# Hybrid diffusion step on one Trainium2 core: modulation row products moved behind whole weight pieces, the expert selection turned with its weights, overflow weights loaded from an earlier point

## The reference

```python
def adaln(cvec, w_mod, b_mod):
    m = jax.nn.silu(cvec) @ w_mod + b_mod
    return [t[:, None, :] for t in jnp.split(m, 6, axis=-1)]

hid = jax.nn.silu(jnp.einsum('nd,edf->nef', x, wg)) * jnp.einsum('nd,edf->nef', x, wu)
y = jnp.einsum('nef,efd->nd', hid * combine[..., None].astype(hid.dtype), wd)
```

## Time and profile before

| | us |
|---|---|
| median of three runs | 2106.62 (2103.02 to 2111.81) |
| the profiled execution, own time | 2109.68 |
| its span | 2107.9 |
| TensorE busy | 1938.4 (92%) |
| VectorE busy | 492.7 (23%) |
| ScalarE busy | 365.7 (17%) |
| mean granted TensorE clock | 0.956 of full |
| weight transfers | 593.40 MB, mean 282 GB/s |

### The profile page before, as it was taken

How to read it: one execution, slowest core, us unless ns; L and a number is a source line. 1 busy time by engine, 2 the same in 40 slices (tenths; PEclk the granted TensorE clock), 3 DMA queues, 4 the chain that set the end, 5 groups by cost and what they waited for, 6 DMA issues and landing times.

```text
span 2107.9 us, 23590 instructions
## 1 busy us (share of the span) xinstructions
PE 1938.4 (92%) x9696; PEld 1154.9 (55%) x9696; DVE 492.7 (23%) x1235; ACT 365.7 (17%) x735; POOL 15.0 (1%) x41
## 2 busy tenths in 40 slices
PE   5877999999999998999999997999999869999987
PEld 2445645545736766855554665744554547555543
DVE  1014411104300322231112334321112042311111
ACT  1013200003103321210002223300002042100002
POOL 1000000000000000000000000000000000000000
PEclk9988999999999978999999997999999988999988
DMA  9882389995997311549999672449999653499970
GB/s 328 311 314 106 153 365 427 428 421 215 351 353 272 120 40 58 201 175 427 428 427 397 235 271 80 180 200 424 429 428 361 228 216 128 163 425 428 428 302 21
DMA packets 126144, 593.40 MB, mean 282 GB/s; under 512 B 8008, under 2 KB 15312, under 8 KB 101088
## 3 DMA queue, kind: packets, MB, share of 16 engines
q1 hardware_dynamic: 115728, 585.12, 69.7%
q10 hardware_dynamic: 9840, 6.52, 1.1%
q0 software_dynamic: 480, 0.39, 0.1%
HBM read 587.29 MB, written 4.73 MB: 281 GB/s over the span
## 4 chain that ended last, share of the span: by engine, by line
PE 85%; DVE 5%; DMA 5%; ACT 4%; issue 2%; ACTq 0%; DVEq 0%; SPq 0%
PE PS L808 24%; PE PS L1249 21%; PE PS L1229 11%; PE PS L1260 10%; PE PS L837 4%; DMA ring<-in_moe_wu 2%; DMA ring<-in_w_mod 2%; PE PS L858 2%; PE PS L989 2%; PE PS L852 2%; ACT arena L591 1%; PE PS L1205 1%; PE PS L873 1%; DVE RS L1385 1%; PE PS L1144 1%
## 5 line engine op out<-in xcount | busy, mean ns | idle before, releaser
L1249 PE MATMUL PS<-ring,arena 128*64 128x512 f32 x1568 | 352.2, 594 | 6.7 <-ACT arena L741 4.3
L1229 PE MATMUL PS<-arena 128*128 128x128 f32 (+3 forms) x1584 | 252.1, 316 | 10.8 <-ACT arena L741 4.4
L1229 PEld LDWEIGHTS PS<-arena 128*128 128x128 f32 (+1 forms) x1584 | 221.3, 194 | 51.9 <-issue 25.0
L808 PE MATMUL PS<-H,ring 128*128 128x256 f32 (+1 forms) x1088 | 248.1, 383 | 1.6 <-DVE SQ L1454 1.6
L1249 PEld LDWEIGHTS PS<-ring,arena 128*64 128x64 f32 x1568 | 119.3, 137 | 231.4 <-issue 226.9
L1260 PE MATMUL PS<-ring,arena 128*64 128x512 f32 x1040 | 235.6, 597 | 4.0 <-DVE arena L1686 4.0
L808 PEld LDWEIGHTS PS<-H,ring 128*128 128x128 f32 x1088 | 203.5, 194 | 54.0 <-issue 28.4
L741 ACT ACTIVATE arena<-PS 128x512 f32<-128x512 f32 (+2 forms) x131 | 71.4, 545 | 899.4 <-PE PS L1260 362.0
L1706 DVE SCALAR_TENSOR_TENSOR arena<-arena,PS 128x512 f32<-128x512 f32 x32 | 35.3, 1104 | 533.4 <-PE PS L1249 533.4
L808 PE MATMUL PS<-arena,ring 128*128 128x256 f32 (+1 forms) x672 | 149.8, 385 | 5.4 <-DVE arena L1529 3.1
L1260 PEld LDWEIGHTS PS<-ring,arena 128*64 128x64 f32 x1040 | 73.0, 137 | 142.1 <-issue 133.5
(11 more groups left out here) (303 smaller groups left out, 1353.7 us busy)
## 6 DMA issues: line engine op xcount, KB each, us to landing
ring<-in_moe_wu SPq DMA_DIRECT2D x65, 2048.0 KB, 16.6
ring<-in_moe_wd SPq DMA_DIRECT2D x65, 2048.0 KB, 11.3
ring<-in_w_mod SPq DMA_DIRECT2D x48, 2048.0 KB, 17.9
ring<-in_moe_wg SPq DMA_DIRECT2D x33, 2048.0 KB, 18.7
arena<-in_moe_wg SPq DMA_DIRECT2D x32, 2048.0 KB, 19.2
ring<-in_mlstm_w_in SPq DMA_DIRECT2D x12, 2048.0 KB, 9.0
ring<-in_attn_w_qkv SPq DMA_DIRECT2D x6, 2048.0 KB, 20.4
ring<-in_gla_w_in SPq DMA_DIRECT2D x6, 2048.0 KB, 10.7
```

The costliest lines, as they stand in the source:

```text
L808: ins = mm(out, a, b, start=first and i == 0, stop=final and i == len(pairs) - 1)
L1229: return mm(out, rows, onehot, start=first, stop=final, skip_group_check=True)
L1249: ins = mm(PS[64 * e:64 * e + 64, b, :], XG[:, k, 64 * e:64 * e + 64], w[:, k], start=(k == 0), stop=(k == KD - 1))
```

## The change

- `MODS[3]` takes 12 pieces (before 8) and `MODS[4]` 4 (before 8): the GLA computes the first eight column blocks of layer 3's modulation, layer 3's attention only the last four.
- `fill` is gone. `mod_run(g, lo, hi)` issues row products after whole weight pieces: in layer 0's attention four after the key/value piece and four after the first query piece; in the mLSTM two after each of eight pieces; in the GLA two after each of six.
- In both attention layers the last four products stand between `scores(0)` and `scores(1)`; `mod_cols` stands after `scores(1)`, ScalarE's `mods` after `probs(0)`, VectorE's after the second maxima.
- In the GLA `mod_cols(3)` and `mods(3)` stand after the eight block products.
- The order of pieces follows: in layer 3 all three `qkv` pieces come before the four modulation pieces.
- `turn_w` transposes WB in place of PB; the two one-column matmuls go, `WTS` has no weight column, and `hid` is a plain product. `scatter` so applies the routing weight.
- The overflow's `wg` and `wu` go to the ring slots that pair 6's `wg` pieces leave, its `wd` to EXTRA's first place (`XWD`). SyncE waits for pair 6's and pair 7's first `up` and no longer for pair 7's second `up` and its `down`.

```diff
-MODS = [ORDER[a:b] for a, b in ((0, 4), (4, 16), (16, 32), (32, 40), (40, 48))]
+MODS = [ORDER[a:b] for a, b in ((0, 4), (4, 16), (16, 32), (32, 44), (44, 48))]
+GMODS = (0, 2, 4, 6, 8, 10, 12)
...
-                chunks += [("gin", 2, c)] + ([("mod", *u) for u in MODS[3][2 * c:2 * c + 2]] if c < 4 else [])
+                chunks += [("gin", 2, c)] + [("mod", *u) for u in MODS[3][GMODS[c]:GMODS[c + 1]]]
...
-            chunks += [("qkv", 3, 2)] + mod(3, 4, 8) + [("qkv", 3, 0)] + mod(3, 8, 12) + [("qkv", 3, 1)] + [("wo", 3, c) for c in range(2)]
+            chunks += [("qkv", 3, c) for c in (2, 0, 1)] + mod(3, 8, 12) + [("wo", 3, c) for c in range(2)]
...
+        XWD = ar(9608, 4, 1024)
...
-                    for j in range(3):
-                        wait(sp, *used(n - 6 + 2 * j))
+                    wait(sp, *used(n - 12))
+                    wait(sp, *used(n - 11))
+                    wait(sp, *used(n - 6))
...
-                            sp.dma_start(slot_view(w, (n - 6 + 2 * j) % RING), expert_weights(w, l, e)).then_inc(S(f"x_landed{j}"), 16)
+                            dst = XWD if w == "wd" else slot_view(w, (n - 6 + j) % RING)
+                            sp.dma_start(dst, expert_weights(w, l, e)).then_inc(S(f"x_landed{j}"), 16)
...
                 probs(0)
+                mods(l + 1)
...
+            def mod_run(g, lo, hi):
+
+                for i in range(lo, hi):
+                    mod_rows(g, i)
...
-                        if fill[m] and k == KD // 2:
-                            mod_rows(*fill[m])
...
+                if l == 0:
+                    mod_run(1, 0, 4)
...
+                    if l == 0 and m == 3:
+                        mod_run(1, 4, 8)
...
-                mod_cols(l + 1)
...
                 scores(0)
+                mod_run(l + 1, len(MODS[l + 1]) - 4, len(MODS[l + 1]))
                 for g in range(KV):
                     n = 4 * a + g
                     if g + 1 < KV:
                         scores(g + 1)
+                    if g == 0:
+                        mod_cols(l + 1)
...
+                    mod_run(2, 2 * c, 2 * c + 2)
...
+                    mod_run(2, 8 + 2 * c, 10 + 2 * c)
...
+                    mod_run(3, GMODS[c], GMODS[c + 1])
...
+                    if s:
+                        mod_run(3, GMODS[2 + i // 2], GMODS[3 + i // 2])
-                mod_cols(3)
...
+                    if i % 4 == 3:
+                        mod_run(3, GMODS[4 + i // 4], GMODS[5 + i // 4])
...
+                mod_cols(3)
                 pe.wait_ge(S("g_r_sb"), 8)
-                pe.wait_ge(S("mod"), mod_done(3))
...
                 def turn_w(b, sem, rows=P):
                     for s in range(2):
-                        tp(PS[0:rows, b, T * s:T * s + T], PB[:, s].rearrange("p e t -> p (e t)")[:, 0:rows], ident)
-                    for s in range(2):
-                        ins = mm(PS[0:rows, b, N2:N2 + 1], WB[:, s].rearrange("p e t -> p (e t)")[:, 0:rows], ones[:, 0:1], start=(s == 0), stop=(s == 1))
+                        ins = tp(PS[0:rows, b, T * s:T * s + T], WB[:, s].rearrange("p e t -> p (e t)")[:, 0:rows], ident)
                     ins.then_inc(S(sem), 1)
...
-                    v.wait_ge(S("wts"), n + 1)
-                    stt(by_k(HID), row(SG), WTS[:, par, N2:N2 + 1], row(bank(here[1])), ALU.mult, ALU.mult).then_inc(S("hid"), 1)
+                    tt(by_k(HID), row(SG), row(bank(here[1])), ALU.mult).then_inc(S("hid"), 1)
```

More of the change, by code:

```diff
@@ L623, in mlstm @@
                 for i in range(8):
+                    act.wait_ge(S("l_v"), i + 1)
+                    run(A(mV[:, i % 2, 512 * (i // 2):512 * (i // 2) + 512], bank(4 + i % 2), ACT.Copy), "l_v_sb")
                     if i == 7:
                         mods(2)
-                    act.wait_ge(S("l_v"), i + 1)
-                    run(A(mV[:, i % 2, 512 * (i // 2):512 * (i // 2) + 512], bank(4 + i % 2), ACT.Copy), "l_v_sb")
                     if i < 2:
@@ L708, in gla @@
                     run(A(gR[:, i], bank(4 + i % 2, 0, N2), ACT.Copy), "g_r_sb")
+                    if i == 7:
+                        mods(3)
                     if i in (3, 4):
@@ L800, in _, with group @@
             mm, tp = pe.matmul, pe.transpose
-            def group(out, pairs, sem=None, first=True, final=True, fill=None):
+            def group(out, pairs, sem=None, first=True, final=True):
                 pairs = list(pairs)
                 for i, (a, b) in enumerate(pairs):
-                    if fill and i == len(pairs) // 2:
-                        mod_rows(*fill)
                     ins = mm(out, a, b, start=first and i == 0, stop=final and i == len(pairs) - 1)
@@ L888, in attention @@
                     pe.wait_ge(*((S("a_k_sb"), 2 * a + m + 1) if m < 2 else (S("a_kv_sb"), 2 * a + m - 1) if m < 4 else (S("a_q_sb"), 8 * a + m - 3)))
-                    group(bank(m % 4, 0, N2), zip(tile(w, m % 4), [H[:, k] for k in range(KD)]), "a_q", fill=fill[4 + m])
+                    group(bank(m % 4, 0, N2), zip(tile(w, m % 4), [H[:, k] for k in range(KD)]), "a_q")
+                    if l == 0 and m == 3:
+                        mod_run(1, 4, 8)
                     if m == 0:
@@ L974, in mlstm @@
                             after(pe, "l_abs")
-                        group(bank(m % 4, 0, N2), zip(tile(w, m % 4), [H[:, k] for k in range(KD)]), "l_qk", fill=(2, m // 2) if m % 2 == 0 else None)
+                        group(bank(m % 4, 0, N2), zip(tile(w, m % 4), [H[:, k] for k in range(KD)]), "l_qk")
+                    mod_run(2, 2 * c, 2 * c + 2)
                 for c in range(4):
@@ L980, in mlstm @@
                         wait(pe, "l_v_sb", i - 1)
-                        group(bank(4 + i % 2), [(H[:, k, T * s:T * s + T], w[:, k]) for k in range(KD)], "l_v", fill=(2, 8 + i))
+                        group(bank(4 + i % 2), [(H[:, k, T * s:T * s + T], w[:, k]) for k in range(KD)], "l_v")
+                    mod_run(2, 8 + 2 * c, 10 + 2 * c)
                 mod_cols(2)
@@ L1108, in qk @@
                         wait(pe, "g_qk_sb", 4 * c + m - 3)
-                        group(bank(m, 0, N2), zip(tile(w, m), [H[:, k] for k in range(KD)]), "g_qk", fill=(3, 2 * c + m // 2) if m % 2 == 0 else None)
+                        group(bank(m, 0, N2), zip(tile(w, m), [H[:, k] for k in range(KD)]), "g_qk")
+                    mod_run(3, GMODS[c], GMODS[c + 1])
                 def gates(lo, hi):
@@ L1130, in gla @@
                     s = i % 2
-                    group(bank(i), [(H[:, k, T * s:T * s + T], w[:, k]) for k in range(KD)], "g_v", fill=(3, 4 + i))
-                mod_cols(3)
+                    group(bank(i), [(H[:, k, T * s:T * s + T], w[:, k]) for k in range(KD)], "g_v")
+                    if s:
+                        mod_run(3, GMODS[2 + i // 2], GMODS[3 + i // 2])
                 pe.wait_ge(S("g_abs"), 2)
@@ L1180, in gla @@
                 after(pe, "g_sm")
+                pe.wait_ge(S("mod"), mod_done(3))
                 for u in range(2):
@@ L1324, in moe @@
                         pe.wait_ge(S("x_landed2"), 16 * before + 16 * i)
-                        down([slot_view("wd", (n0 + 46) % RING)], 0, 4)
-                        down([slot_view("wd", (n0 + 46) % RING)], 1, 5).then_inc(S("x_down"), 1)
+                        down([XWD], 0, 4)
+                        down([XWD], 1, 5).then_inc(S("x_down"), 1)
                         pe.wait_ge(S("scatter"), q0 + 8)
@@ L1557, in gla @@
                 diff(0)
-                mods(3)
                 v.wait_ge(S("g_qk_sb"), 8)
@@ L1763, in moe @@
                         v.wait_ge(S("x_turn_w"), before + i)
-                        copy(WTS[0:64, 0, 0:N2 + 1], PS[0:64, 5, 0:N2 + 1], "x_wts", before + i)
+                        copy(WTS[0:64, 0, 0:N2], PS[0:64, 5, 0:N2], "x_wts", before + i)
                         v.wait_ge(S("x_gather"), before + i)
```

16 lines of the change are left out of this document (5 added, 11 removed).

## The result

The changed kernel takes 2050.07 us (median of four runs, 2046.77 to 2052.38), the kernel before in the same session 2104.82; the ratio is 0.9732, with a 95% interval of 0.9705 to 0.9759. The profiled execution took 2051.54 with a span of 2049.7, against 2109.68 and 2107.9: 58.1 us, where the sum had 56.4.

The account below looks back on a forecast made before the run. TensorE was taken as the bound, 85% of the chain. -26.3 - 1.0 - 24.9 - 1.0 - 1.5 + 2.5 - 3.7 - 0.5 = -56.4 us gave 2053.3 profiled, 2050 on the median; range 2036 to 2064.

Parts of the forecast that it names:

- the cores: Attention cores, layers 0 and 3: the last four products fit TensorE's 8.04 us gap; -1.0 us in each layer.
- the turned selection: Mixture of experts: two one-column matmuls go, 0.34 us a turn, but the weight stream limits the gain; -3.7 us.
- the mLSTM: Layer 1: 16 isolated products become eight runs of two, while ScalarE's copy loses its cover; -1.5 us.
- the GLA: Layer 2: 12 products and not 8, with the 2.78 us wait before the first block product covered; +2.5 us.
- the projections of layers 0 and 3: Attention projections: stalls, low clock and isolated products go, product runs come in; -26.3 us in layer 0, -24.9 in layer 3.
- The stalls and the ring: Attention projections: TensorE's waits for modulation pieces, 7.02 and 6.33 us in layer 0 and 6.85 in layer 3, go.
- My argument for layer 3: Layer 3's projections: both query pieces are among the first three, so no stall replaces the old 6.85 us.
- A product's price: Modulation products: an isolated one costs 1.99 us, 1.72 of it its four steps.
- The change of shape: Modulation products: switching matmul shape in and out costs 0.27 us, paid only by the first product in a run.
- The rival that the core keeps the upper clock: Attention cores: the filled gap keeps the upper clock, 5 us in all, mostly in layer 3; 2045 us, chance 15%.
- `hid`: Mixture of experts: VectorE's operation loses its scalar operand; 0, at most -0.4 us for each of five.
- The overflow: Layer 3's overflow expert: loads were hidden already, so earlier loads give 0; the transposed selection's turn gives -0.5 us.

Follow-up runs that it names:

- run 9: The changed kernel with layer 0's first eight row products back inside the key, value and query groups, one at a time: 2058.55 us.
- run 10: The changed kernel with four row products moved back from the GLA to layer 3's attention: 2050.78 us.
- run 4: The changed kernel with the mLSTM's 16 row products back inside groups, one at a time, and ScalarE's copy back before the last value group's: 2048.82 us.
- 2: The kernel before with the turned selection alone: 2101.78 us, ratio 0.9979.
- 5: The kernel before, loading only half of the down weights of pairs 1 to 7 in each layer: 2110.92 us, ratio 1.0013.
- 6: The kernel before with half of the down weights of pairs 1 to 7 left out, plus the turned selection: 2090.39 us.
- 1: The changed kernel's row products alone, with the old expert selection and old overflow loads: 2049.28 us, ratio 0.9731 to the kernel before.
- 7: The changed kernel with expert weight pieces going round four double slots (three in the ring, one EXTRA), so loads are issued earlier: 2040.77 us.
- run 11: The changed kernel with the old overflow loads, all three issued after the last pair's last down product: 2050.80 us.
- run 8: The changed kernel with eight unread matmuls added in each of the four waits for the copied probabilities in both attention cores: 2051.66 us.

## Why the prediction was right, step by step

**The total** came out at 2050.07 for 2050, which is partly luck. The forecast took 56.4 off a median of 2106.62; the kernel before had 2104.82 beside the result, so the medians fell by 54.8 and the profiled executions by 58.1. Inside the 58.1 errors cancelled: the cores were 4.0 and 0.8 us worse than forecast; the turned selection was 1.9 better, the mLSTM 1.9 and the GLA 1.7 by their stages, the projections of layers 0 and 3 1.0 and 0.8; the clock's level alone gave 2.0 in layer 3's output projection and took 1.9 at the end and 0.8 in layer 0's first sum of squares.

**The stalls and the ring.** Right in place and size: -27.3 and -25.7 for -26.3 and -24.9. That the place of a product in relation to the slot's release makes the stall is shown for layer 0's first one by run 9; for the second and for layer 3's it is argued from the same rows. My argument for layer 3, that both query pieces had to be among the first three, named more than was needed (run 10).

**A product's price.** The step of 1.72 held. The change of shape was mis-sized both ways: from one instruction's start to the next, a run of four takes 7.00 and a run of two 3.57, so 0.14 is the change in and out of a run and not 0.27; and a merged pair saves 0.32 (run 4).

**The cores.** This term of -1.0 each is not borne out: +3.0 and -0.2. The first wait shrank as forecast: the first exponentials began 4.9 us behind the last rotation where it was 5.8. VectorE's four `mods` operations before the copies held up the values' product and with it the third scores, so that the third maxima waited 0.63 us for TensorE (141.29), where before they did not wait; yet the fourth scores still began 1.4 us earlier behind the last rotation than before. The loss comes from there on, where the same instructions ran at the lower level. First the kernel before, then the changed one:

```profile
176.53 0.50 PE L918 MATMUL PS<-arena 64*128 64x128 f32 x4
...
188.37 1.53 PE L932 MATMUL PS<-consts,arena 128*128 128x128 f32 x12 [2.40 <-DVE arena L1438]
```

```profile
148.56 0.81 PE L926 MATMUL PS<-arena 64*128 64x128 f32 x4 [0.54 <-ACT small L597]
...
161.81 2.82 PE L943 MATMUL PS<-consts,arena 128*128 128x128 f32 x12 [3.98 <-DVE arena L1453]
```

The last transposes begin 42.9 us behind the last rotation in both, and the output projection then begins 3.0 later. How much of this is the change can't be told from one trace of each. In the four kernels with the old core (before, runs 2, 5 and 6) layer 0's core, from the first scores to the output projection, took 48.0, 48.0, 51.1 and 51.0 us, with a granted clock of 0.82 in the two short ones and 0.73 in the others. In six with the new core (the change, runs 1, 4, 7, 10 and 11) it took 50.5 to 51.8 at 0.80. So most of the +3.0 is that the trace before had caught a short one; against the other two the change is level. Layer 3's core took 50.6 to 50.7 before and 49.0 to 51.3 after. What makes the clock fall earlier in some executions stays open. The rival that the core keeps the upper clock did not come true: in layer 3 the granted clock rose from 0.74 to 0.81 while the core got 0.2 us shorter, and with 1.00 (run 8) the two cores still took 50.2 and 49.7.

**mLSTM and GLA.** From the gates to `mod_cols` the mLSTM lost 1.9 (forecast 1.5, whose shape changes were 0.05 too cheap). The other 1.5 of the stage lies behind, in parts that the change doesn't touch, and is no effect that one trace can show: that part took 228.7 to 235.0 us in the nine kernels with runs of two. The GLA's stretch grew by 1.4 and not 2.5, since a run of two took 3.57, and 3.47 in front of a block product, and not 3.71: 1.0 for six runs.

**The turned selection.** The mechanism was right: the stream takes back most of it. Three runs show it from three sides: 1.5 a stage with the full stream (2), 3.2 a stage with a lighter (6) and, with the whole change, 2.0 to 2.3 a stage more when the loads are issued earlier (7). The term was mis-sized, because I took a turn at the chain's 0.34 and a period fell by 0.45. The four stages gave 1.1 to 1.9 each, 6.1 in all, for a forecast of 4.2 (3.7 and 0.5 for the overflow's turn); two turns ahead of the stream's start at 0.45 make 0.9 of each, the rest is slack at the last pair, which was argued and not tested. `hid` went from 1104 to 1047 ns, worth nothing.

**The overflow.** Right: nothing (run 11).

## What to carry to other kernels

A row product between matmuls of another shape costs its own time plus some 0.3 us, and one that is wanted right after the slot of its own piece is given back costs most of a load's latency (a wait of 7.0 us for a load of 8.7): put such work behind whole pieces, so that each wanted piece is one piece's work behind the release. Work with no deadline belongs into the longest gap of TensorE, where a run of 7.0 us was free but for 0.5; that it also keeps the clock up for what follows is what one pair of traces shows, at 1 to 2 us. Before shaving TensorE's loop, hold its period against the bytes it needs: here 29.07 us against 29.4 meant that a saving of 13 us showed as 6 until the loads were issued earlier.

## What the runs showed that I had not expected

The same instructions take different times from run to run and from kernel to kernel by where TensorE's clock falls. The output projection of layer 0 took 27.89 us in nine of the fourteen traces and 29.6 to 29.8 in the other five, that of the double slots among them; layer 3's expert stage from its last pair's turn on varied from 57.3 to 60.8 us, with 0.5 of it for the overflow's turn; the end, untouched, from 13.2 to 15.6; the mLSTM behind `mod_cols` by more than 6. So one execution's stage is known to 2 us or worse wherever TensorE has been idle, and stages of dense matmuls to 0.1: the experts' stage of 260.5 repeated to 0.02 in nine readings. A term of 1 us in such a stage, as mine for the cores, can't be checked with one trace before and one after.
